# Chunked delta rule: one stream of four heads, or two streams of two heads each, on TensorE, VectorE and ScalarE

## What is computed

```python
u = rms_norm(h); cols = u @ w_in
h = h + concat(ssd(A), rglru(B), rwkv7(C), nsa(D)) @ w_out
h = h + peer(rms_norm(h))
```

```python
def step(state, inp):                      # state: 64 x 64 per head
    r_t, w_t, k_t, v_t, kk_t, a_t = inp
    sa = einsum('bhij,bhj->bhi', state, -kk_t)
    state = (state * w_t[:, :, None, :] + sa[..., None] * (kk_t * a_t)[:, :, None, :]
             + v_t[..., None] * k_t[:, :, None, :])
    y_t = einsum('bhij,bhj->bhi', state, r_t)
```

## Time and profile before

| | us |
|---|---|
| median of 3 runs | 3880.43 (3870.2 to 3882.09) |
| the profiled execution | 3892.06 |
| its span, first to last instruction | 3890.4 |
| PE / PEld busy | 3244.4 (83%) / 2271.2 (58%) |
| DVE / ACT / POOL busy | 2461.6 (63%) / 852.0 (22%) / 895.0 (23%) |
| mean granted TensorE clock | 0.908 |

### The profile page before, as it was taken

One profiled execution on the slowest core, in us unless ns is written; L12 is line 12 of the kernel. 1 busy time (PEld: TensorE's weight loads), 2 busy tenths in 40 slices (PEclk: granted clock), 3 DMA queues, 4 the chain that ended last, 5 costly groups with the idle time before them and its releaser, 6 DMA issues. The chain is left out here.

```text
span 3890.4 us, 39693 instructions
## 1 busy us (share of the span) xinstructions
PE 3244.4 (83%) x13220; PEld 2271.2 (58%) x13220; DVE 2461.6 (63%) x5162; ACT 852.0 (22%) x1940; POOL 895.0 (23%) x856
## 2 busy tenths in 40 slices
PE   6937777877799999999678478777777999999995
PEld 5725566765466666666266255666654666666662
DVE  3573553887686666666646634548866866666666
ACT  2331223127500000000033313221365000000000
POOL 0011201216522222222100122012255222222221
PEclk9968878989899999999889788788888999999997
DMA  3100112169999999999831001121699999999997
GB/s 102 54 0 1 48 33 76 63 219 321 328 393 417 417 417 414 409 415 401 319 97 38 1 1 48 44 77 65 232 317 359 386 416 417 417 416 416 415 403 288
DMA packets 235344, 943.33 MB, mean 242 GB/s; under 512 B 19584, under 2 KB 85632, under 8 KB 164864
## 3 DMA queue, kind: packets, MB, share of 16 engines
q0 software_dynamic: 73728, 536.90, 34.1%
q1 hardware_dynamic: 95360, 370.31, 25.0%
q10 hardware_dynamic: 66048, 33.56, 3.0%
HBM read 904.52 MB, written 35.65 MB: 242 GB/s over the span
## 5 line engine op out<-in xcount | busy, mean ns | idle before, releaser
L1881 PE MATMUL bank<-peer_x_late,xT 128*128 128x256 f32 x4096 | 941.7, 384 | 93.6 <-ACT peer_acts_u L1947 49.9
L1881 PEld LDWEIGHTS bank<-peer_x_late,xT 128*128 128x128 f32 x4096 | 788.7, 193 | 305.8 <-issue 153.0
L2009 DVE CUSTOM_DVE_ANT_0 peer_slots<-peer_slots,wide 128x1024 f32<-128x1024 f32 x512 | 627.8, 1227 | 516.5 <-DMA peer_slots<-in_peer_uv,peer_rows 514.9
L1829 POOL DMA_INDIRECT peer_slots<-in_peer_uv,peer_rows x512 | 534.6, 1044 | 1444.7 <-DVE h L2020 1295.2
L1901 PE MATMUL bank<-ring,peer_acts_u 128*128 128x512 f32 x1280 | 584.8, 601 | 38.4 <-DVE peer_acts_u L2040 29.7
L2020 DVE SCALAR_TENSOR_TENSOR h<-peer_slots,peer_coef,h 128x1024 f32<-128x1024 f32 x416 | 533.7, 1283 | 7.6
L1901 PEld LDWEIGHTS bank<-ring,peer_acts_u 128*128 128x128 f32 x1280 | 245.8, 193 | 294.8 <-issue 283.9
L1901 PE MATMUL bank<-ring,wide 128*128 128x512 f32 x768 | 347.1, 597 | 8.5 <-DMA ring<-in_peer_uv 8.4
L1901 PEld LDWEIGHTS bank<-ring,wide 128*128 128x128 f32 x768 | 146.7, 191 | 161.7 <-issue 146.5
L1870 PE MATMUL bank<-peer_hot 128*128 128x128 f32 x1024 | 154.8, 301 | 77.7 <-ACT peer_hot L1954 77.4
L1870 PEld LDWEIGHTS bank<-peer_hot 128*128 128x128 f32 x1024 | 142.1, 210 | 132.2 <-ACT peer_hot L1954 117.0
(11 more groups left out here) (459 smaller groups left out, 4206.3 us busy)
## 6 DMA issues: line engine op xcount, KB each, us to landing
xT<-in_peer_ut SPq DMA_DIRECT2D x256, 512.0 KB, 16.5
ring<-in_peer_uv SPq DMA_DIRECT2D x256, 512.0 KB, 16.1
gates<-peer_staging ACTq DMA_DIRECT2D x32, 1024.0 KB, 16.0
peer_staging<-gates SPq DMA_DIRECT2D x32, 1024.0 KB, 17.9
ring<-in_w_in SPq DMA_DIRECT2D x48, 512.0 KB, 3.6
ring<-in_peer_wq SPq DMA_DIRECT2D x32, 512.0 KB, 3.6
nsa_w<-in_cmp_w SPq DMA_DIRECT2D x2, 4096.0 KB, 12.1
ring<-in_w_out SPq DMA_DIRECT2D x16, 512.0 KB, 4.3
```

What stands on the lines that cost most here:

```text
L1829: nc.gpsimd.indirect_dma_start(out=p.slots[:, n % ROW_SLOTS, :], out_offset=None, in_=A["peer_uv"], in_offset=bass.IndirectOffsetOnAxis(ap ...
L1881: last = nc.tensor.matmul(k.bank[bank_of[j]][:, 0:DENSE], u_raw[:, j % U_RING, b * P:(b + 1) * P], p.x_late[:, b, :], start=b == 0, stop=b ...
L2009: nc.vector.tensor_tensor_reduce(out=u, in0=u, in1=k.wide[:, t, :], scale=1.0, scalar=0.0, op0=ALU.mult, op1=ALU.add, accum_out=p.dots[:, ...
```

## The change

Only `rwkv_chunks` changes. The four heads are split into two pairs `i` = 0 and 1. Each pair gets its own semaphores (`product0`, `product1`, `dve_kept0` and so on; 13 in the stage in place of 9), three banks X, Y, Z for its products, and one bank V (6 or 7) for its transpositions, which in between takes the products that bank 5 (and bank 3 for `bv`) took. Every step on every engine is done for pair 0, then for pair 1. The matmuls keep their number, shapes and operands. DVE and ACT instructions that handled four heads (128x512) become two that handle two (128x256), and ACT's 128x256 become 128x128; those of DVE that already went by pairs stay. In the last steps `ta` writes both its results for a pair into Y (it was banks 1 and 2), the local output goes to Z (it was bank 4) and `local` to X (it was bank 3). The unused semaphore `masked` goes, and the wait for `zeroed` stands only before the first tile.

```diff
+    of_pair = lambda i: slice(2 * i, 2 * i + 2)
+    mid = lambda i: (k.bank[3 * i], k.bank[3 * i + 1], k.bank[3 * i + 2], k.bank[6 + i])
...
             for t in range(TT):
-                if t:
-                    dve_did(pe, "h", t - 1)
-                    act_did(pe, "y", t - 1)
-                for i in range(2):
-                    mm(k.bank[0][:, i * 256:(i + 1) * 256], r.alpha[:, i, c], r.b_pad[:, i, :, c], start=True, stop=True)
-                    mm(k.bank[1 + i][:, :], r.beta[:, i, c], r.a_pad[:, i, :, c], start=True, stop=True)
-                    last = mm(k.bank[3 + i][:, :], r.kappa[:, i, c], r.a_pad[:, i, :, c], start=True, stop=True)
-                last.then_inc(s["product"], 1)
-                dve_did(pe, "n", t)
-                for h in range(4):
-                    o = slice(h * P, (h + 1) * P)
-                    mm(k.bank[0][:, o], NT[:, h, :], N[:, h, :], start=True, stop=True)
-                    last = mm(k.bank[5][:, o], N[:, h, :], NT[:, h, :], start=True, stop=True)
-                last.then_inc(s["product"], 1)
+                for i in pairs:
+                    X, Y, Z, V = mid(i)
+                    if t:
+                        dve_did(pe, i, "h", t - 1)
+                        act_did(pe, i, "y", t - 1)
+                    mm(X[:, 0:256], r.alpha[:, i, c], r.b_pad[:, i, :, c], start=True, stop=True)
+                    mm(Y[:, :], r.beta[:, i, c], r.a_pad[:, i, :, c], start=True, stop=True)
+                    mm(Z[:, :], r.kappa[:, i, c], r.a_pad[:, i, :, c], start=True, stop=True).then_inc(s[f"product{i}"], 1)
+                for i in pairs:
+                    X, Y, Z, V = mid(i)
+                    dve_did(pe, i, "n", t)
+                    act_did(pe, i, "turn", t)
+                    for h, o, q in of_heads(i):
+                        mm(X[:, o], NT[:, h, :], N[:, h, :], start=True, stop=True)
+                        last = mm(V[:, o], N[:, h, :], NT[:, h, :], start=True, stop=True)
+                    last.then_inc(s[f"product{i}"], 1)
...
@@ vector
-                nc.vector.tensor_copy(N2, four(0))
-                tt(IN2, four(0), ident4, ALU.add).then_inc(s["dve_kept"], 1)
-                for i in range(2):
-                    hh = slice(2 * i, 2 * i + 2)
-                    tt(A16[:, hh, :], two(1 + i, 0), bc(mk[:, 2, :], 2), ALU.mult)
-                    tt(A32[:, hh, :], two(1 + i, 0), bc(mk[:, 3, :], 2), ALU.mult)
-                    last = tt(D[:, hh, :], two(1 + i, 256), bc(mk[:, 5, :], 2), ALU.mult)
-                last.then_inc(s["dve_kept"], 1)
+                for i in pairs:
+                    X, Y, Z, V = mid(i)
+                    hh = of_pair(i)
+                    pe_did(dve, i, "n2", t)
+                    nc.vector.tensor_copy(N2[:, hh, :], two(X, 0))
+                    tt(IN2[:, hh, :], two(X, 0), ident2, ALU.add).then_inc(s[f"dve_kept{i}"], 1)
+                    tt(A16[:, hh, :], two(Y, 0), bc(mk[:, 2, :]), ALU.mult)
+                    tt(A32[:, hh, :], two(Y, 0), bc(mk[:, 3, :]), ALU.mult)
+                    tt(D[:, hh, :], two(Y, 256), bc(mk[:, 5, :]), ALU.mult).then_inc(s[f"dve_kept{i}"], 1)
...
@@ scalar
-                pe_did(act, "w", t)
-                cp(W, four(0)).then_inc(s["act_kept"], 1)
-                pe_did(act, "w2", t)
-                cp(W, four(0)).then_inc(s["act_kept"], 1)
+                for after_step in ("w", "w2"):
+                    for i in pairs:
+                        pe_did(act, i, after_step, t)
+                        cp(W[:, of_pair(i), :], two(mid(i)[2], 0)).then_inc(s[f"act_kept{i}"], 1)
```

More of the change, by code:

```diff
@@ L852, in after @@
         engine.wait_ge(sem, t * len(steps) + steps.index(name) + 1)
[L854 to L858, removed]
+    with stage(nc, "zeroed", "dve_done", "act_done",
+               *[f"{name}{i}" for i in range(2) for name in ("turned", "product", "dve_kept", "act_kept", "pool_kept")]) as (block, s):
+        pe_did = lambda e, i, name, t: after(e, s[f"product{i}"], PE_STEPS, name, t)
+        dve_did = lambda e, i, name, t: after(e, s[f"dve_kept{i}"], DVE_STEPS, name, t)
+        act_did = lambda e, i, name, t: after(e, s[f"act_kept{i}"], ACT_STEPS, name, t)
+        pool_did = lambda e, i, name, t: after(e, s[f"pool_kept{i}"], POOL_STEPS, name, t)
+        pairs = range(2)
         @block.tensor
@@ new lines, in _ @@
+                for i in pairs:
+                    X, Y, Z, V = mid(i)
+                    dve_did(pe, i, "tq2", t)
+                    for h, o, q in of_heads(i):
+                        last = mm(Z[:, o], A32[:, h, :], T2[:, h, :], start=True, stop=True)
+                    last.then_inc(s[f"product{i}"], 1)
+                for i in pairs:
+                    X, Y, Z, V = mid(i)
+                    act_did(pe, i, "w2", t)
+                    for h, o, q in of_heads(i):
+                        last = mm(V[:, o], W[:, h, :], Q2[:, h, :], start=True, stop=True)
+                    last.then_inc(s[f"product{i}"], 1)
@@ L949, in _ @@
+                for i in pairs:
+                    X, Y, Z, V = mid(i)
+                    pool_did(pe, i, "u", t)
+                    for h, o, q in of_heads(i):
+                        mm(X[q, 0:256], r.kapT[:, h, :], r.v_c[:, h, :, :].rearrange("p c d -> p (c d)"), start=True, stop=False)
+                        last = mm(X[q, 0:256], r.betT[:, h, :], r.u_c[:, h, :, :].rearrange("p c d -> p (c d)"), start=False, stop=True)
+                    last.then_inc(s[f"product{i}"], 1)
         @block.vector
@@ L964, in _ @@
                 c = slice(t * P, (t + 1) * P)
-                pe_did(dve, "gram", t)
-                step(tt(N, four(0), bc(mk[:, 0, :], 4), ALU.mult))
-                for i in range(2):
-                    last = tt(NT[:, 2 * i:2 * i + 2, :], two(1 + i, 0), bc(mk[:, 1, :], 2), ALU.mult)
-                last.then_inc(s["dve_kept"], 1)
-                dve_did(dve, "n", t)
-                tt(INT, NT, ident4, ALU.add).then_inc(s["dve_kept"], 1)
-                pe_did(dve, "n2", t)
-                nc.vector.tensor_copy(N2, four(0))
@@ L1001, in _ @@
-                for i in range(2):
-                    gp = k.bank[2][:, i * 256:(i + 1) * 256].rearrange("p (c v) -> p c v", c=4)
+                for i in pairs:
+                    X, Y, Z, V = mid(i)
+                    hh = of_pair(i)
+                    pe_did(dve, i, "gram", t)
+                    step(tt(N[:, hh, :], two(X, 0), bc(mk[:, 0, :]), ALU.mult))
+                    tt(NT[:, hh, :], two(Y, 0), bc(mk[:, 1, :]), ALU.mult).then_inc(s[f"dve_kept{i}"], 1)
+                    dve_did(dve, i, "n", t)
+                    tt(INT[:, hh, :], NT[:, hh, :], ident2, ALU.add).then_inc(s[f"dve_kept{i}"], 1)
@@ L1003, in _ @@
+                if t == 0:
+                    dve.wait_ge(s["zeroed"], 1)
+                for i in pairs:
+                    X, Y, Z, V = mid(i)
+                    pe_did(dve, i, "ta", t)
+                    step(tt(r.rho[:, i, c], r.rho[:, i, c], Y[:, 0:P], ALU.subtract))
+                    gp = Y[:, P:3 * P].rearrange("p (c v) -> p c v", c=4)
                     for e in range(2):
@@ new lines, in _ @@
+                for i in pairs:
+                    hh, Z = of_pair(i), mid(i)[2]
+                    pe_did(act, i, "ut", t)
+                    step(nc.scalar.activation(r.uT[:, hh, :], two(Z, 0)[:, :, 0:64], ACT.Copy, scale=-1.0))
+                    cp(r.taT[:, hh, :], two(Z, 0)[:, :, 64:128]).then_inc(s[f"act_kept{i}"], 1)
+                for i in pairs:
+                    pe_did(act, i, "ta", t)
+                    cp(k.mixed[:, 4 + i, c], mid(i)[2][:, 0:P]).then_inc(s[f"act_kept{i}"], 1)
```

249 lines of the change are left out of this document (124 added, 125 removed).

## The result

The changed kernel takes 3794.28 us in the median of 4 runs (3790.44 to 3802.3) against 3880.01 (3870.2 to 3882.09): ratio 0.977, 95% interval 0.9747 to 0.9794, so 85.7 us less. The profiled execution took 3802.3 us with a span of 3800.6, 89.8 us under that of before. The forecast was 3788 us, 92.3 us less.

A forecast was written before the change was run, and what follows sets the result against it. No engine is full; PE and its helpers take turns in a chain. Rounds of 25.6 us plus 0.7 save 46.4 us a layer, 92.8 in two, less 0.5 for barriers: 92.3, so 3788 us, range 3771 to 3817.

The forecast's parts named there:

- PE's own work: PE's matmuls and transpositions in a round, at full clock: 22.7 us, unchanged by the split.
- Handovers: PE's waits and tails between steps: 11.5 us a round shrinks to 2.4, covered by the other pair's work.
- the seam: Passage from `local` to the next round's `gram`: 0.3 us of wait left.
- Clock: PE's clock in the stage: full except at the start; low clock had cost 13.1 us a layer, gain 12.4.
- rival 1: PE's clock falls as before because work stays light, giving back 2 x 12.4 us: 3813 us; chance 0.15.
- low stretches: Five times in a layer of the old kernel with PE at the 1.2 GHz level, 28 us in all.
- the one at 317.2: Clock fall after the 2.48 us wait before `gram`, said to agree with the skill's long idle gaps.
- the start: First round of a layer, where low clock was to cost the same 0.7 us a layer as before.
- Rival 2: DVE starts each instruction only after the one before is through, 0.42 not 0.33 us: 3797 us; chance 0.10.
- Barrier: Stage's end: four more semaphores cleared at 0.057 us each, costing 0.23 us a layer.
- Rival 3: No overlap: PE's waits for a pair hold for both, 11.5 us a round stays: 3892 us or nothing; chance 0.02.
- Rival 4: PE stays at 1.2 GHz through the stage, 181.6 us a layer, 32 more than before: 3945 us; chance 0.03.

The follow-up runs named there:

- PE locked at every step: The changed kernel with PE waiting for both pairs at every step before it starts pair 0: 3867.4 us, ratio 0.9935.
- warm: The changed kernel with five unused 512-column products at the end of PE's list in the stage before: 3808.4 us, ratio 0.9813.
- warm7: The changed kernel with seven unused 512-column products at the end of PE's list in the stage before: 3795.8 us, ratio 0.9779.
- locked late: The changed kernel with PE waiting for both pairs only in the steps from `w` to the next `gram`: 3841.1 us, ratio 0.9869.

## Why the prediction was right

**PE's own work** of 22.7 us a round stayed, and no engine took its place as the bound: DVE 15.1 and ACT 7.9 of 25.9.

**Handovers.** Forecast 2.4 us left, 25.1 a round, raised to 25.6; measured 25.9. The forecast's remainders are counted from start to start, tails included; so counted, PE's timeline of the second round has 3.2 us beyond the steady pace, and 25.9 - 3.2 is the 22.7. Most came out where the list had them: 0.66 before pair 1's `n4` (0.65), 0.33 before pair 0's `tq` (0.3), 0.34 before pair 1's `w2` (0.35) and 0.31 before pair 0's (0.2), 0.25 before pair 1's `n2` (0.2). The one that was short is the seam, 0.70 against 0.3. Its terms there, 0.2 + 0.86 + 0.05 - 0.9, add up to 0.2 and not 0.3, and they leave out that DVE is still on `rho` and G of pair 1 when H of pair 0 could start, as the rows of the seam show: the same kind of order as at `n4`, which the forecast had seen. The run with `gram`'s product into X last bears it out, 0.5 us a round.

**Clock.** 1.00 from the second round on, and rival 1 (it falls as before) was refuted. The run that held it in the kernel before puts its worth at 11 to 12 us a layer, the forecast's 12.4; that is 2 x 12.4 of 92.3, a good quarter and not the third that the forecast named. Its 28 us of low stretches were read short too: the clocks 0.86, 0.87 and 0.87 of the earlier trace rows make 30.6. With PE locked at every step the clock fell after waits of 1.13 and 0.55 us between light steps, while 1.98 us without work at the barrier, after dense work, left it up. The Trainium skill's account of long idle gaps, in "TensorE: Matmul & The Clock Gate", section "HAM oscillation — how this bites in real kernels", does not reach these falls, nor quite the one at 317.2 behind 2.48 us that the prediction gave to it; the fall in the 3.8 us gap of `warm` is of its kind. The page as a whole is not against them, though: its section "A second HAM failure mode: psum-queue depth-cycling" has the clock swing, in a bf16 kernel, from short idle times between groups of matmuls, and the rows of the locked run are nearer to that.

**The term that was mis-sized** is the start: 0.7 us a layer was taken from the first round of before, and it cost 2.0 (27.9 against 25.9). With 0.3 for each of the rounds, and the last one's further 0.25, this makes the stage 105.8 and not 103.1 us, and the two layers 87.4 and not 92.8. The profiled executions differ by 89.8, so 2.4 us came from outside the stage, where nothing was changed; that the totals lie so near the forecast is in part luck. The medians' 85.7 can't be split like this, since the runs of one kernel range over 12 us.

**Starts on DVE.** Rival 2 (0.42 apart) is out: they are 0.33 apart wherever the next instruction doesn't wait for the one before. With it goes the strict reading of the Trainium skill's "VectorE: DVE Perf Modes", section "Terms", that the next operation can't issue until the pipeline is empty. Still, without overlap the kernel with the halved instructions took 4 us a round more.

**Barrier.** From DVE's end at 386.38 to its next start at 387.67 are 1.29 us with 13 semaphores, 1.05 before with 9: the 0.23 forecast.

**Rivals 3 and 4.** Rival 3's mechanism, PE's waits in effect for both pairs, was made by hand: 3867 us, 23 under the kernel before and not 12 over it, because DVE and ACT still overlap with PE. Only with their waits locked too does it cost more than that, 3927 us. Rival 4 didn't come; the lowest clock over a round of any run here is 0.81.

## What to carry to other kernels

Where one engine alternates with its helpers in a chain and each step handles several independent items, two streams over the same instruction lists can cover most of the waits, here 9.9 us a round to 1.3; what then remained was set in good part by the order on the in-order helper queue, so put what the other stream's next product needs ahead of what is needed later. Here the chain with waits on TensorE paid twice, in the waits and in the clock of the work between them; products that nobody needs, shorter than the wait that they stand in, tell in one run how much of the time is clock. Small effects in a long program are read from the stage, where rounds at the full clock repeat to 0.02 us, not from whole runs that differ by 10.

## What was not expected

The clock is not a function of the work alone. The changed kernel's first round is 27.9 us at 0.93 or 0.94 in all of its traces, but in the run with the later masks the same beginning gave 27.24 us at 0.93 in layer 1 and 26.08 at 0.97 in layer 2:

```profile
282.55:309.79 27.24, 26.00 (x174) 20.08 (x173) 15.57 (x42) 8.49 (x29) 12.53 (x13) 0.93 0.00 1
2169.01:2195.09 26.08, 24.92 (x174) 19.63 (x173) 15.07 (x42) 8.49 (x29) 12.34 (x13) 0.97 0.00 1
```

The low level of the start lasted on into the round, 3.8 us behind the first product of `gram` in the one and 1.5 in the other. In all traces it is one of these two, 1.3 to 1.5 or 3.4 to 3.9 us (none in `warm7`): the short one in both layers of the kernel before and in layer 1 of the run with its clock held up, the long one in layer 2 of that same run and in every layer of the changed kernel's two traces. The same rounds of layer 2 in the run that was locked late differ by 2.6 us. A cost of 1 to 3 us can so appear or vanish between two otherwise equal stages, and one round is no base for its price: the 0.7 us of the forecast was such a draw.
